# One transformer kernel on one core: attention layers reordered, six modulation units moved from VectorE to TensorE

## What is computed

```
h = rmsnorm(x, norm1_g[i]) * (1 + scale1) + shift1
i == 0: q, k, v = split(h @ w_qkv); rotate the first 16 of each 64 of q and k
        w = softmax(q1 k1^T / 8) - lam * softmax(q2 k2^T / 8)      8 heads of 2 x 64, values of 128
        o = rmsnorm(w @ v) * subln_g * (1 - lam_init)
i == 1: 8 query heads of 128, 2 key and value heads; q and k are rmsnormed and rotated
        o = softmax(q k^T / sqrt(128)) @ v
x = x + gate1 * (o @ w_o)
h = rmsnorm(x, norm2_g[i]) * (1 + scale2) + shift2
x = x + gate2 * ((silu(h @ w_gate) * (h @ w_up)) @ w_out)           inner width 2816
```

## Time and profile before

| what | value |
|---|---|
| median of 3 runs | 1319.41 us (1317.56 to 1320.39) |
| the profiled execution | 1320.98 us, of it span 1319.2 us |
| TensorE busy | 1123.8 us (85%) |
| VectorE busy | 674.1 us (51%) |
| ScalarE busy | 545.1 us (41%) |
| mean granted TensorE clock | 0.956 of full speed |
| DMA | 397 MB, mean 301 GB/s |

### The profile page before, as it was taken

The page is one execution under the profiler, slowest core; times in us unless marked ns, Lnnn a source line. Parts: engine busy times, 40 slices in busy tenths (PEclk is TensorE's granted clock), DMA queues, the critical chain, the costliest instruction groups (busy, mean ns, idle before and its releaser), DMA issues.

```text
span 1319.2 us, 19883 instructions
## 1 busy us (share of the span) xinstructions
PE 1123.8 (85%) x8439; PEld 845.6 (64%) x8439; DVE 674.1 (51%) x1415; ACT 545.1 (41%) x1185; POOL 0.2 (0%) x4
## 2 busy tenths in 40 slices
PE   6999999867666675757799889999999979999997
PEld 5777667534333442424467667788887758788886
DVE  4575665111111010101077776898886865777765
ACT  4554554111111111101155654666644754666653
POOL 0000000000000000000000000000000000000000
PEclk9999999989897988889899989999999999999999
DMA  9996947999999999999997416686757613655500
GB/s 388 424 425 250 391 158 296 429 426 427 427 426 428 423 427 428 427 427 426 427 390 297 192 64 238 267 320 251 310 209 297 247 64 132 251 192 192 192 32 32
DMA packets 29702, 397.36 MB, mean 301 GB/s; under 512 B 3496, under 2 KB 4904, under 8 KB 5416
## 3 DMA queue, kind: packets, MB, share of 16 engines
q1 hardware_dynamic: 29176, 395.72, 73.3%
q10 hardware_dynamic: 432, 0.30, 0.1%
HBM read 394.97 MB, written 1.05 MB: 300 GB/s over the span
## 4 chain that ended last, share of the span: by engine, by line
PE 55%; DMA 23%; DVE 13%; ACT 7%; issue 1%; DVEq 0%; ACTq 0%
PE ps L1161 16%; DMA ring<-in_w13b 12%; PE ps L1165 8%; DMA mem<-in_w13b 6%; PE ps L1155 5%; PE ps L1157 4%; PE ps L1156 4%; ACT mem L1863 4%; DVE memr L2364 4%; PE ps L1691 4%; DMA ring<-in_w13a 3%; ACT memr L1863 3%; DVE mem L2364 2%; PE ps L1651 2%; PE ps L1195 2%; PE ps L1746 2%
## 5 line engine op out<-in xcount | busy, mean ns | idle before, releaser
L2364 DVE TENSOR_TENSOR memr<-ring,memr 128x512 fp32r<-128x512 f32 x432 | 292.0, 689 | 166.1 <-ACT memr L1863 162.8
L1863 ACT ACTIVATE memr<-ring 128x512 fp32r<-128x512 f32 x432 | 264.5, 628 | 176.9 <-PE ps L1157 67.7
L1863 ACT ACTIVATE mem<-ps 128x512 f32<-128x512 f32 (+5 forms) x307 | 128.2, 438 | 393.5 <-PE ps L1691 236.7
L1161 PE MATMUL ps<-memr 128*128 128x512 f32 x1056 | 275.3, 394 | 3.4 <-DVE memr L2364 2.1
L1161 PEld LDWEIGHTS ps<-memr 128*128 128x128 f32 x1056 | 186.7, 189 | 36.5 <-DVE memr L2370 5.1
L1155 PE MATMUL ps<-memr 128*128 128x256 f32 (+2 forms) x504 | 180.1, 357 | 6.6 <-DVE memr L2364 4.1
L2364 DVE TENSOR_TENSOR mem<-mem,ps 128x512 f32<-128x512 f32 (+1 forms) x76 | 43.5, 572 | 248.1 <-ACT mem L1863 248.0
L1156 PE MATMUL ps<-memr 128*128 128x256 f32 (+2 forms) x504 | 165.9, 329 | 0.0
L1157 PE MATMUL ps<-memr 128*128 128x256 f32 (+2 forms) x504 | 165.8, 329 | 0.0
L1165 PEld LDWEIGHTS ps<-memr 128*128 128x128 f32 x1056 | 151.4, 190 | 16.5 <-DVE memr L2370 0.9
L1165 PE MATMUL ps<-memr 128*128 128x256 f32 x1056 | 156.9, 282 | 0.9 <-DVE memr L2370 0.5
(11 more groups left out here) (180 smaller groups left out, 1039.7 us busy)
## 6 DMA issues: line engine op xcount, KB each, us to landing
ring<-in_wpk SPq DMA_DIRECT2D x89, 2048.0 KB, 9.7
ring<-in_w13a SPq DMA_DIRECT2D x17, 2048.0 KB, 44.8
mem<-in_w13b SPq DMA_DIRECT2D x16, 2048.0 KB, 45.8
ring<-in_w SPq DMA_DIRECT2D x16, 2048.0 KB, 45.2
ring<-in_w13b SPq DMA_DIRECT2D x16, 2048.0 KB, 42.9
mem<-in_w13a SPq DMA_DIRECT2D x15, 2048.0 KB, 45.4
mem<-in_w SPq DMA_DIRECT2D x15, 2048.0 KB, 45.6
mem<-in_wpk SPq DMA_DIRECT2D x1, 2048.0 KB, 10.4
```

The source lines that it names most:

```text
L1161: return self.e.matmul(ps[:, 0:512], a[0], b[1], start=start, stop=stop)
L1863: return self.e.activation(out, src, f, **k)
L2364: return self.e.tensor_tensor(out, a, b, op)
```

## The change

- Second layer: queries and keys are packed into four units of two heads each (`qk0` to `qk3`: 256 query and 256 key columns), followed by v0 and v1. `qk` results are transposed by `turn_both`, queries by ScalarE with the factor 0.125, keys by VectorE.
- The scores (`scores_pair`, 18 steps, one every second slab) and the values (`values_pair`, 10 steps) are two generators. The transposed weights of all eight heads are kept (`e2T1` has eight buffers).
- Units (1,7), (1,8) and (1,9) go from VectorE to TensorE, between the units of the second layer.
- Third layer: kv2 is first, then q20, then q21. q20's `norm_rope` is taken two steps a slab beside q21; the first three attention steps stand beside the end of q21, nine stand bare.
- Units (2,6), (2,7) and (2,8) go from VectorE (in the feed-forward before) to TensorE, after the bare steps 4, 6 and 9 of the third layer.
- Four units stay on VectorE, one chunk every 6 slabs. There are ten groups of units on TensorE in place of eight.

```diff
-       ((1, 4), (1, 5), (1, 6)), ((1, 11), (2, 0), (2, 1)),
-       ((2, 4), (2, 5)), ((2, 10), (2, 11)))
-TURNED_AT = (0, 2, 4, 5, 7, 9, 11)
-TURNED_1 = ((1, 7), (1, 8), (1, 9))
-TURNED_2 = ((1, 10), (2, 2), (2, 3), (2, 6), (2, 7), (2, 8), (2, 9))
+       ((1, 4), (1, 5), (1, 6), (1, 7)), ((1, 8), (1, 9)), ((1, 11), (2, 0), (2, 1)),
+       ((2, 4), (2, 5)), ((2, 6), (2, 7), (2, 8)), ((2, 10), (2, 11)))
+TURNED_AT = (0, 3, 6, 9)
+TURNED = ((1, 10), (2, 2), (2, 3), (2, 9))
...
+        self.e2T1 = [span(o + 512 * j, 2, 256) for o in (15360, 12288, 10240, 11264) for j in range(2)]
...
+    def turn_both(self, tag, src, ready, g):
+        yield
+        yield
+        self.turn_pair(tag, 0, src, ready, self.m.qT1[:, 2 * g:2 * g + 2, :], 0.125, self.a_free)
+        yield
+        self.turn_pair(tag, 2, src, ready, self.m.kT1[:, 2 * g:2 * g + 2, :], 1.0, self.a_free)
+        yield
...
+    def scores_pair(self):
+        for step in range(18):
+            if step < 16 and step % 2 == 0:
+                self.a_scores(1, step // 2)
+            if 1 <= step < 17:
+                self.a_weigh(1, step - 1)
+            if 2 <= step:
+                self.a_turn(1, step - 2)
+            yield
+    def values_pair(self):
+        for h in range(0, 8, 4):
+            for n in range(5):
+                if n:
+                    self.a_end(1, h + n - 1)
+                if n < 4:
+                    self.a_values(1, h + n)
+                yield
...
     def layer2
-        self.slow = self.turned_units(TURNED_1, 5)
         self.side.append(self.second_norm())
-        qk_unit("q10", 0, 0.125, m.qT1, 0, self.a_free)
+        qk_unit(0)
+        self.side.append(self.paced(self.scores_pair(), [5] + [1] * 17))
+        self.side.append(self.paced(self.values_pair(), [32, 1, 0, 1, 0, 1, 1, 1, 1, 0]))
         self.ada_unit(1, 5)
-        qk_unit("k10", 1, 1.0, m.kT1, 0, self.a_free)
+        qk_unit(1)
         self.ada_unit(1, 6)
+        qk_unit(2)
+        self.ada_unit(1, 7)
+        qk_unit(3)
         v_unit(0)
-        self.side.append(self.paced(at, [1] * 8))
-        qk_unit("q11", 2, 0.125, m.qT1, 1, self.a_free)
-        qk_unit("k11", 0, 1.0, m.kT1, 1, self.turned("q10"))
-        self.side.append(self.paced(at, [4, 0, 0, 0]))
+        self.ada_unit(1, 8)
         v_unit(1)
-        self.drain()
-        next(at)
-        self.side.append(self.paced(at, [0] * 9))
+        self.ada_unit(1, 9)
...
     def layer3
+        self.project("kv2", m.h2, low)
+        self.copy_kv()
+        self.side.append(self.chain(*[rope("kv2", m.kvb[:, tt, 0:256], 2, 1, tt, tt) for tt in range(2)],
+                                    self.turn("kv2", m.kvb, [(s.dve_att, ("nr", "kv2", 1))], m.kT2, n=2, free=self.a_free)))
         self.project("q20", m.h2, low)
         self.copy_q("q20", m.qst2[0])
-        self.project("kv2", m.h2, low)
-        self.copy_kv()
         self.drain()
+        first_q = self.chain(*[rope("q20", m.qst2[0][:, tt, :], 4, 0, tt, 2 + tt) for tt in range(2)],
+                             self.turn("q20", m.qst2[0], [(s.dve_att, ("nr", "q20", 1))], m.qT2[:, 0:4, :], free=self.a_free))
+        self.side += [first_q, first_q]
+        self.side.append(self.paced(at, [5, 0, 0]))
         self.project("q21", m.h2, low)
         self.copy_q("q21", m.qst2[1])
         last = self.last
         self.drain()
-        for step in range(12):
+        for step in range(3, 12):
...
             next(at)
+            if step in (4, 6, 9):
+                self.ada_unit(2, {4: 6, 6: 7, 9: 8}[step])
+            next(last_q, None)
             next(last_q, None)
```

More of the change, by code:

```diff
@@ L325, in __init__ @@
         self.vb, self.qT1, self.kT1 = span(4096, 2, 1024), span(6144, 8, 256), span(8192, 8, 256)
-        self.qst1 = [span(10240 + 1024 * j, 2, 512) for j in range(3)]
-        self.e21, self.e2T1 = span(13312, 4, 2, 256), span(15360, 2, 2, 256)
+        self.qst1 = [span(10240 + 1024 * j, 2, 512) for j in range(2)]
+        self.e21 = span(13312, 4, 2, 256)
+        self.e2T1 = [span(o + 512 * j, 2, 256) for o in (15360, 12288, 10240, 11264) for j in range(2)]
         self.oB1 = span(23448, 2, 256)
@@ L737, in turn, with turn_on_act @@
         for c2 in range(0, n, 2):
-            self.turn_pair(tag, c2, src, ready, dst, scale, free)
+            self.turn_pair(tag, c2, src, ready, dst[:, c2:c2 + 2, :], scale, free)
             yield
+    def turn_both(self, tag, src, ready, g):
[5 more added lines that the diff above has]
+        yield
+    def turn_on_act(self, tag, c2, scale):
+        return c2 == 0 if tag[:2] == "qk" else c2 % 4 or scale != 1.0
     def turned(self, tag, n=4, scale=1.0):
-        on_act = lambda c2: c2 % 4 or scale != 1.0
-        return [(self.s.act_att if on_act(c2) else self.s.dve_att, ("turn", tag, c2)) for c2 in range(0, n, 2)]
+        return [(self.s.act_att if self.turn_on_act(tag, c2, scale) else self.s.dve_att, ("turn", tag, c2))
+                for c2 in range(0, n, 2)]
     def attention_first(self):
@@ L882, in second_norm_part, with layer2, qk_unit @@
         yield
-    def layer2(self, at):
+    def layer2(self):
         m, s = self.m, self.s
         low = lambda k: (s.dve_h, ("low", (1, 0), k))
-        def qk_unit(tag, slot, scale, dst, g, free):
+        def qk_unit(g):
+            tag, store = f"qk{g}", m.qst1[g % 2]
             self.project(tag, m.h2, low)
-            self.rope1(tag, m.qst1[slot], scale, free)
-            self.side.append(self.turn(tag, m.qst1[slot], [(s.dve_att, ("rope", tag, 1))], dst[:, 4 * g:4 * g + 4, :], waits=2,
-                                       free=self.a_free))
+            self.rope1(tag, store, 1.0, self.a_free if g < 2 else self.turned(f"qk{g - 2}"))
+            self.side.append(self.turn_both(tag, store, [(s.dve_att, ("rope", tag, 1))], g))
         def v_unit(g):
@@ L1059, in stages @@
     for i in (1, 2):
-        at = p.attention(i)
+        at = p.attention_last() if i == 2 else iter(())
         if i == 1:
-            p.layer2(at)
+            p.layer2()
         else:
@@ L1084, in stages @@
         if i == 1:
-            p.slow = p.turned_units(TURNED_2, 4)
+            p.slow = p.turned_units(TURNED, 6)
         for n in range(11):
@@ L1536, in a_scores @@
         if i == 1:
-            ready = self.turned(f"q1{h // 4}") + self.turned(f"k1{h // 4}")
+            ready = self.turned(f"qk{h // 2}")
         else:
@@ L2671, in turn_pair @@
         w, s, m = self.w, self.s, self.m
-        if not c2 % 4 and scale == 1.0:
+        if not self.turn_on_act(tag, c2, scale):
             w.wait_ge(s.pe_att, ("turn", tag, c2))
```

54 lines of the change are left out of this document (24 added, 30 removed).

## The result

The kernel after takes 1322.77 us (median of 19 runs, 1321.88 to 1325.82), the kernel before 1319.23 us beside it (19 runs, 1317.56 to 1321.49). The ratio is 1.0028, its 95% interval 1.0022 to 1.0035: 3.5 us lost, where 1.0 us won was forecast. The profiled execution of after took 1322.0 us, its span 1320.1 us, at a mean granted clock of 0.952.

A forecast was written before the change was run, and what follows sets the result against it. TensorE was taken to set the pace, busy 85% of the span, with gaps in the attention stages. Terms -6.8, -0.4 and +6.2 summed to -1.0 us, giving 1318.4 us; range 1312.5 to 1323.5.

The forecast's parts named there:

- Second layer: Second layer's attention: idle time and slow clock won back, less remaining waits and the units' price; 6.8 us won.
- 15.1 less 3.1, 2.0 and 1.0: Second layer's attention: TensorE idle 15.1 us, less untouched waits 3.1, norm-sum and head waits 2.0, small missed waits 1.0.
- Feed-forward: Second layer's feed-forward: TensorE's waits are 1.25 us, mostly not of VectorE's chunks; 0.4 us won, between 0 and 1.2.
- Third layer: Third layer's attention: a new 4.6 us wait ahead of q20's transposes, units included; 6.2 us lost, bounds 1.6 and 10.0.
- The keys' transposes, priced at 0.4 us: Third layer's attention: transposes of the keys, added to the layer's length at 0.4 us with no wait.
- The slow clock, priced at 1.0 us: Third layer's attention: 1.0 us lost to slow clock after the long wait ahead of q20's transposes.
- q21 itself, laid out at 18.3 us: Third layer: q21's slabs 10.9, wait 4.6, transposes 0.8, two heads' scores 1.8, one transpose 0.2; 18.3 us.
- A: Rival, third layer: bare steps give back q21's wait and gaps absorb all units; 0.5 us lost, 1312.7 us; chance 0.27.
- B: Rival, third layer: clock falls inside q21 and stays down, costing 4 to 5 us; 1323.4 us; chance 0.17.
- C: Rival, second layer: chains form again, only 6 of 15.1 us idle go, won 0.3; 1324.9 us; chance 0.07.
- The lower bound of 1 us for the second layer: Second layer's attention: only 1 us won if half of the others' 12.0 us of waits form again.
- with every unit paid in full, 10.0: Third layer's attention, upper bound of the loss: units not absorbed by waits, 3.8 us more, 10.0 us lost.

The follow-up runs named there:

- run 13: Kernel after, with q20's transposes after slab six of q21 instead of four and the scores two slabs later: 1319.7 us, ratio 0.9995 to the kernel before.
- run 12: Kernel after, with the third layer's key transposes one slab later: 1322.37 us, ratio 1.002 to the kernel before.
- run 14: Kernel after, with key transposes one slab later and 15 unread matmuls in the wait ahead of q20's transposes: 1319.84 us, ratio 0.9999 to the kernel before.
- run 7: Kernel after, with 15 unread 128x128 matmuls filling the wait ahead of q20's transposes: 1321.85 us, ratio 1.0013 to the kernel before.
- run 2: Kernel before, with only the third layer changed as in the kernel after: 1329.07 us, ratio 1.0062 to the kernel before.
- run 8: Kernel after, with the second layer's scores one slab later: 1323.09 us, ratio 1.0024 to the kernel before.
- run 3: Kernel after, with the third layer's three units back on VectorE in the feed-forward, its new order kept: 1325.23 us, ratio 1.0034 to the kernel before.
- run 10: Kernel after, with the second layer's scores one slab later and the third layer as in the kernel before: 1313.19 us, ratio 0.9949 to the kernel before.
- run 11: Kernel after, second layer's scores one slab later, third layer as before with unread matmuls in two bare-step waits: 1312.69 us, ratio 0.9946 to the kernel before.
- run 1: Kernel after, with the third layer's order and units as in the kernel before: 1314.52 us, ratio 0.996 to the kernel before.
- run 15: Kernel after, second layer's scores, values and norm sums one slab later, third layer as before with two bare waits filled: 1314.97 us, ratio 0.9959 to the kernel before.

## Why the prediction was wrong

**Second layer (predicted -6.8, measured -7.05): right in its main reason, and in the sum with some luck.** The transposes' waits behind VectorE fell to 0.7 us (forecast: small). TensorE's idle time fell by 7.7 us where 15.1 less 3.1, 2.0 and 1.0 made 9.0, and the clock gave back all 5.1 us where 4.1 were forecast; the two misses nearly cancel. The single wait of 1.4 us at the second norm sum did not come: the norm sums and the values wait 1.4 us in three pieces of at most 0.5. In its place stand the two waits of 1.3 us for the turned keys, which are in none of its terms. A sign missed too: the output projection was to start 6 to 7 us earlier, and it started 0.6 us earlier (109.2 us after the layer's first slab, before 109.7). The rest of the gain lies behind that point, where before waited 3.5 us for the last heads and was at the lower clock until 786 us. The reason given, that VectorE is relieved of chunks and of the ends of earlier heads together, is what the corners show: the order alone gives 0.1 us and the relief alone 2.7.

**Feed-forward (predicted -0.4, measured -1.3): a little more than the upper bound of 1.2.** I took most of its waits for none of the chunks'. Three fewer chunked units, in every kernel that has them, give 1.2 to 1.5 us. VectorE's busy time there fell by 11.9 us, where 15 were forecast.

**Third layer (predicted +6.2, measured +10.2): this is the step that failed, by size.** Its mechanism is there: one wait of 4.77 us (4.6 forecast) after four slabs of q21, ended by VectorE, and it is a loss by itself (run 13). The bare steps after the third took 21.4 us, from 1061.3 to 1082.7 (21.1 forecast). The output projection started 9.8 us later against the layer's first slab (68.8 against 59.0), where 4 to 6 were forecast. The two signs that the prediction named for itself being wrong, this wait below 2 us or the second layer's transposes still at 4 us, did not come up. The 4.0 us lie in three terms:

- *The keys' transposes, priced at 0.4 us.* "With the keys' transposes 0.4" took them for free of waits. But keys first puts them one slab ahead of q20's end, where VectorE's rotation of kv2 has just ended. They waited 1.78 us (VectorE's last rotation of kv2 ends at 1038.2, the transposes start at 1038.28). From the first slab to q21's start, at 1040.2, the layer lost 2.4 us, 2.0 more than in the sum. One slab later the wait is gone (runs 12 and 14: 1.5 us).
- *The slow clock, priced at 1.0 us.* It cost 1.7 us in this execution (run 7 gives 1.6), and 0.9 to 1.0 us more in runs 2 and 8.
- *q21 itself, laid out at 18.3 us.* It took 21.1, from 1040.2 to 1061.3: 1.7 for the clock, 0.5 for waits 0.2 and 0.3 longer than laid out, 0.6 not placed.

These make 2.0, then 2.8 less the 1.0 of clock in the sum, and 0.3 in the bare steps: 4.1. The sum's 0.6 for the group was 0.4 (41.60 against 41.16 us in the output projection's part). Added to the -1.0 us of the forecast, the three stages' misses give the profiles' +1.9; of the 1.6 us from there to the medians' +3.5, no row shows the cause beyond the 0.9 of clock.

The units were not the fault. I had two of three absorbed by waits; run 3 has them at no cost in the new order, where their price without waits would be 6.3. What the sum left out is that without them the clock falls in the bare steps.

**The rivals.** A (the third layer gains too) is excluded by 110.4 us. B gives nearly the measured time, 1323.4, by another cause: its clock loss of 4 to 5 us was 1.7 in after and 2.6 to 2.7, as time, in runs 2 and 8, and TensorE was back at 2.4 GHz before 1056 us. By the section "HAM oscillation" of the Trainium skill's page "TensorE: Matmul & The Clock Gate" gaps put the clock back to half, and the penalty is half of the time spent there; the trace agrees, with half clock behind the 4.77 us and 1.7 us lost. It didn't stay down, as I had made of it in that rival. C (nothing hidden in the second layer) is excluded by 149.5 us; its price has a slip, since 6 us of waits less 6.3 for the units are 0.3 lost and not "won 0.3". The lower bound of 1 us for the second layer does not follow either: with half of the 12.0 us back, its terms give 4.8 with the clock won and -0.3 without. The measured time lies inside the range, on the wrong side of before. The sign was missed because the upper bound of the third layer, "with every unit paid in full, 10.0", was built from the units, while the terms that were off, the keys and the clock, had no range of their own; 10.2 us came without the units being paid.

**Why the order costs 11 us.** In the old order VectorE's chain of q20 lies under the slabs of kv2, nine slabs ahead of its transposes, and the short chain of kv2 under q21. In the new order the short chain lies under q20 and the long one under four slabs of q21. Of the 11.0 us, measured with the units on VectorE, 7.1 are idle time and 3.9 busy time at the lower clock (run 3). Runs 13 and 14, with the units on TensorE, take 2.7 and 3.1 us away. That they would add up was not tried, and since both touch the stretch behind q20's wait they need not.

## To carry to other kernels

Move a projection only with its chain: for each unit, write down what turns it, how long the side engines take for that, and how many slabs stand before the transposes; the short chain belongs where few slabs follow, the long one where many do. Work moved between engines has no price of its own: the same three units cost 4.4 us in one order and, within 1 us, nothing in the other, and relief of VectorE gave 2.7 or 7 us. So measure the corners (order, placement) apart before both are kept: here the second layer's half alone, with its scores one slab later, takes 1313.2 us, 0.5% less than before (run 10).

## What was not expected of the hardware

The same wait costs different amounts of clock. Behind the 4.8 us wait the clock lost 1.7 us in after (third layer 110.4 us) and 3.4 us in runs 2 and 8 with the same code in that layer (111.4, 111.3), part of it while TensorE still stood. A wait of 1.8 us in the second layer was followed by a loss of 1.7 us in run 11 (149.0 us) and by none in run 10 (147.7 us). Nor does a shorter wait cost less: 2.1 us in run 13 lost the same 1.7. The 17 profiles have 25 stretches of the lower clock between 672 and 1124 us. Added up as above, in windows of 2 us, each lost 1.7 us of clock or 3.4 us, and none a value between.

What it costs in time depends on what stands behind it. Two waits of 1.57 and 1.72 us with 0.44 us of transposes between them, in the bare steps of run 1, were enough for a stretch at half clock:

```profile
1058.00:1060.00 2.00, 1.38 (x5) 1.20 (x6) 1.74 (x6) 1.66 (x8) 0.00 (x0) 0.73 0.00 0
1060.00:1062.00 2.00, 2.00 (x7) 1.52 (x7) 2.00 (x6) 1.62 (x11) 0.00 (x0) 0.50 0.03 8
1062.00:1064.00 2.00, 2.00 (x12) 1.63 (x11) 1.47 (x5) 1.70 (x7) 0.00 (x0) 0.91 0.00 0
```

That stretch lost 1.7 us of clock and none of time (run 11 filled it and the layer stayed at 100.2 us), with VectorE busy 5.2 of the 6 us. The same loss a few microseconds later, just ahead of the output projection, came with a layer 0.9 to 1.0 us longer (runs 10 and 15), and the one behind q20's wait, where cut slabs stood ready, lost 1.6 us of time.
